# Large matmuls that read and write their 512 columns as two interleaved halves, with stationary arrays moved by 64 to 192 bytes

## The reference, cut to what matters

```
proj = rms_norm(x) @ gla_w_in       # 2048 -> 6160
x   += o @ gla_w_out                # 2048 -> 2048
x   += (silu(g) * u) @ ffn_w_out    # g, u = split(rms_norm(x) @ ffn_w_in): 2048 -> 2 * 5632, then 5632 -> 2048, twice
kv   = rms_norm(x) @ w_kv           # 2048 -> 4096
q    = rms_norm(x) @ diff_w_q       # 2048 -> 2048
x   += attention @ diff_w_out       # 2048 -> 2048
```

## Time and profile before

| what | value |
|---|---|
| median of the runs | 2196.01 us (2 runs, 2195.74 to 2196.29) |
| span of the profiled execution, first to last instruction | 2193.8 us |
| time of a run outside that span | 2.2 us (the median less the span) |
| TensorE busy | 2188.1 us, 9720 matmuls |
| weight loads busy | 1808.9 us |
| VectorE, ScalarE, GpSimd busy | 1242.7, 1058.2, 283.0 us |
| moved by DMA | 447.01 MB, mean 204 GB/s |

### The profile page before, as it was taken

The page is one execution under the profiler, slowest core; times in us unless marked ns, Lnnn a source line. Parts: engine busy times, 40 slices in busy tenths (PEclk is TensorE's granted clock), DMA queues, the critical chain, the costliest instruction groups (busy, mean ns, idle before and its releaser), DMA issues.

```text
span 2193.8 us, 27239 instructions
## 1 busy us (share of the span) xinstructions
PE 2188.1 (100%) x9720; PEld 1808.9 (82%) x9720; DVE 1242.7 (57%) x1460; ACT 1058.2 (48%) x1428; POOL 283.0 (13%) x563
## 2 busy tenths in 40 slices
PE   9999999999999999999999999999999999999999
PEld 7888788888888888888888888888888888888887
DVE  5665566655555555555566676665555555555443
ACT  6666455444444444444456665554444444444333
POOL 3210334100000000001125333341000000000000
PEclk9999999999999999999999999999999999999999
DMA  8765667666666666666667666676666666666664
GB/s 264 210 189 176 189 202 218 203 215 203 203 202 213 201 202 206 200 205 203 201 202 217 196 207 202 204 223 210 199 207 200 215 200 203 205 210 194 195 193 163
DMA packets 252675, 447.01 MB, mean 204 GB/s; under 512 B 27665, under 2 KB 41969, under 8 KB 252593
## 3 DMA queue, kind: packets, MB, share of 16 engines
q1 hardware_dynamic: 236176, 428.79, 62.2%
q0 software_dynamic: 16240, 17.07, 2.7%
q10 hardware_dynamic: 176, 0.07, 0.0%
HBM read 414.37 MB, written 2.10 MB: 190 GB/s over the span
## 4 chain that ended last, share of the span: by engine, by line
PE 100%; DVE 0%; ACT 0%; issue 0%; POOL 0%; DVEq 0%; ACTq 0%; POOLq 0%
PE acc L641 32%; PE acc L639 32%; PE acc L640 32%; PE acc L651 1%; PE acc L656 0%; PE side L884 0%; PE tps L678 0%; PE side L727 0%; PE side L703 0%; PE side L762 0%; PE side L882 0%; PE side L898 0%; PE side L899 0%; PE side L900 0%; PE side L782 0%; PE side L780 0%
## 5 line engine op out<-in xcount | busy, mean ns | idle before, releaser
L1311 DVE TENSOR_TENSOR w_lo<-raw,w_hi 128x1024 fp32r<-128x1024 f32 x784 | 954.8, 1222 | 835.6 <-ACT w_hi L945 831.3
L945 ACT ACTIVATE w_hi<-raw 128x1024 fp32r<-128x1024 f32 x784 | 827.8, 1059 | 1002.9 <-PE acc L641 994.0
L639 PE MATMUL acc<-w_hi,xT 128*128 128x512 f32 x2016 | 787.6, 391 | 0.0
L641 PE MATMUL acc<-w_hi,xT 128*128 128x512 f32 x2016 | 784.4, 389 | 0.0
L640 PE MATMUL acc<-w_lo,xT 128*128 128x512 f32 x2016 | 784.4, 389 | 0.0
L639 PEld LDWEIGHTS acc<-w_hi,xT 128*128 128x128 f32 x2016 | 378.4, 188 | 79.0 <-issue 0.7
L640 PEld LDWEIGHTS acc<-w_lo,xT 128*128 128x128 f32 x2016 | 378.4, 188 | 78.9 <-issue 0.7
L641 PEld LDWEIGHTS acc<-w_hi,xT 128*128 128x128 f32 x2016 | 378.4, 188 | 78.9
L639 PE MATMUL acc<-w_hi,hT 128*128 128x512 f32 x700 | 272.3, 389 | 0.0
L640 PE MATMUL acc<-w_lo,hT 128*128 128x512 f32 x700 | 272.3, 389 | 0.0
L641 PE MATMUL acc<-w_hi,hT 128*128 128x512 f32 x700 | 272.3, 389 | 0.0
(11 more groups left out here) (204 smaller groups left out, 1372.2 us busy)
## 6 DMA issues: line engine op xcount, KB each, us to landing
raw<-in_ffn_w_in SPq DMA_DIRECT2D x352, 512.0 KB, 3.8
raw<-in_ffn_w_out SPq DMA_DIRECT2D x176, 512.0 KB, 4.7
raw<-in_gla_w_in SPq DMA_DIRECT2D x96, 512.0 KB, 4.3
raw<-in_w_kv SPq DMA_DIRECT2D x64, 512.0 KB, 4.6
raw<-in_gla_w_out SPq DMA_DIRECT2D x32, 512.0 KB, 4.9
raw<-in_diff_w_q SPq DMA_DIRECT2D x32, 512.0 KB, 4.6
raw<-in_diff_w_out SPq DMA_DIRECT2D x32, 512.0 KB, 4.9
tok<-scratch SPq DMA_DIRECT2D x352, 32.0 KB, 2.9
```

What stands on the lines that cost most here:

```text
L639: nc.tensor.matmul(acc[p][tb][:, :], hi, w_hi[:, slot, j, :], start=(kt + j == 0), stop=False)
L641: last = nc.tensor.matmul(acc[p][tb][:, :], lo, w_hi[:, slot, j, :], start=False, stop=(kt + j == n_kt - 1))
L945: nc.scalar.activation(w_hi[:, slot, :, :], raw[:, slot, :, :], ACT.Copy).then_inc(hi_done, 1)
L1311: nc.vector.tensor_tensor(w_lo[:, slot, :, :], raw[:, slot, :, :], w_hi[:, slot, :, :].bitcast(F32), ALU.subtract).then_inc(lo_done, 1)
```

## The change

In `unit`, the moving operand (`w_hi`, `w_lo`) and the output bank are seen as two halves of 256 columns, which are walked in turn: c columns of the low half, c of the high half, the next c of the low half, and so on. Input and output are walked alike, so each product still lands in its own column. The number c depends on the phase: 4, 8, 16 or 32. `first_unit` and `last_unit` keep the straight walk. The number, order and operands of the matmuls and weight loads stay, as do all waits and DMAs. Beside that, the arrays `g_oT`, `hT`, `xT_q` and `d_oT` start at 64, 128, 128 and 192 bytes modulo 512, in place of 0; `xT` stays at 0. What lies behind them in SBUF (`x_turned`, `q_squares`, `p_squares`, `p_turned`) moves along.

```diff
-            place("gap_g", 0, s1)
+            place("gap_g", 64, s1)
             g_oT = sb("g_oT", [P, 2, KT, S], F32R, s1)
...
-            place("gap_h", 0, s1)
+            place("gap_h", 128, s1)
             hT = sb("hT", [P, 2, FKT, S], F32R, s1)
...
-            place("gap_d", 0, s1)
+            place("gap_q", 128, s1)
             with ExitStack() as s2:
                 xT_q = sb("xT_q", [P, 2, KT, S], F32R, s2)
+            place("gap_d", 192, s1)
             d_oT = sb("d_oT", [P, 2, KT, S], F32R, s1)
...
+            chunk = {'gla_in': 16, 'gla_out': 16, 'ffn_in0': 4, 'ffn_out0': 16, 'diff_in': 8, 'diff_q': 8, 'diff_out': 16, 'ffn_in1': 32, 'ffn_out1': 4}
+
+            def halves(row, c):
+
+                if c == CB:
+                    return row
+                return row.rearrange("q (h m c) -> q m h c", h=2, c=c)
+
-            def unit(src, kt, n_kt, p, slot, u):
+            def unit(src, kt, n_kt, p, slot, u, c=CB):
...
-                        nc.tensor.matmul(acc[p][tb][:, :], hi, w_hi[:, slot, j, :], start=(kt + j == 0), stop=False)
-                        nc.tensor.matmul(acc[p][tb][:, :], hi, w_lo[:, slot, j, :], start=False, stop=False)
-                        last = nc.tensor.matmul(acc[p][tb][:, :], lo, w_hi[:, slot, j, :], start=False,
-                                                stop=(kt + j == n_kt - 1))
+                        at, high, low = (halves(row, c) for row in (acc[p][tb][:, :], w_hi[:, slot, j, :], w_lo[:, slot, j, :]))
+                        nc.tensor.matmul(at, hi, high, start=(kt + j == 0), stop=False)
+                        nc.tensor.matmul(at, hi, low, start=False, stop=False)
+                        last = nc.tensor.matmul(at, lo, high, start=False, stop=(kt + j == n_kt - 1))
```

More of the change, by code:

```diff
@@ L819, in _ @@
                     u = UNIT0["gla_in"] + b * UB + k
-                    (first_unit if b == 0 else unit)(xT, 2 * k, KT, b % 2, u % SLOTS, u)
+                    if b == 0:
+                        first_unit(xT, 2 * k, KT, b % 2, u % SLOTS, u)
+                    else:
+                        unit(xT, 2 * k, KT, b % 2, u % SLOTS, u, chunk["gla_in"])
             def out_phase(phase, src, n_kt, units, before, src_job=None):
@@ L833, in out_phase @@
                     u = UNIT0[phase] + at
-                    (last_unit if u == UNITS - 1 else unit)(src, 2 * k, n_kt, b % 2, u % SLOTS, u)
+                    if u == UNITS - 1:
+                        last_unit(src, 2 * k, n_kt, b % 2, u % SLOTS, u)
+                    else:
+                        unit(src, 2 * k, n_kt, b % 2, u % SLOTS, u, chunk[phase])
             def turn_x(phase, b, x_name):
@@ L856, in ffn_pair @@
                         pe.wait_ge(evacuated[half], TB * (BLOCK0[phase] // 2) + TB * i)
-                    unit(xT, 2 * k, KT, half, at % SLOTS, UNIT0[phase] + 2 * UB * i + at)
+                    unit(xT, 2 * k, KT, half, at % SLOTS, UNIT0[phase] + 2 * UB * i + at, chunk[phase])
             def ffn(layer, x_name):
@@ L921, in _ @@
                     u = UNIT0["diff_in"] + b * UB + k
-                    unit(xT_q if 4 <= b < 8 else xT, 2 * k, KT, b % 2, u % SLOTS, u)
+                    if 4 <= b < 8:
+                        unit(xT_q, 2 * k, KT, b % 2, u % SLOTS, u, chunk["diff_q"])
+                    else:
+                        unit(xT, 2 * k, KT, b % 2, u % SLOTS, u, chunk["diff_in"])
             def diff_tail(at):
```

## The result

The changed kernel takes 2347.57 us (2 runs, 2347.55 to 2347.59) against 2196.01 before: a ratio of 1.069, with a 95% interval of 1.066 to 1.072. It is 152 us slower, where I forecast 70 us faster, and lies outside the range.

A forecast was written before the change was run, and what follows sets the result against it. TensorE's matmul pace was taken as the bound. From the 2193.8 us span, 70 us was taken off for the moving operand's walk, other parts adding nothing; with 2.2 us around it, 2126 us, range 2090 to 2215.

The forecast's parts named there:

- What bounds the kernel: Whole kernel: TensorE is busy for 2188.1 of 2193.8 us, so time is number of matmuls times distance between starts, 226.7 ns.
- What the 13.3 ns is made of: Each wide matmul's excess over 213.3 ns streaming: 2 ns fixed cost, 11.4 ns moving stream held up by the weight load.
- The walk of the moving operand: Reads of w_hi and w_lo in halves keep in step with the load: 7.5 ns gained on 9300 matmuls, 70 us.
- The walk of the output: PSUM bank written in pieces, smallest four float32: taken as costing nothing, though no row gave a price.
- my slow rival: The rival "Breaks cost", with 0.42 ns at each break of the output walk; chance 0.08.
- The new offsets: Stationary arrays moved to 64, 128 or 192 bytes: 3252 matmuls, plus or minus 4.4 ns, included in the 7.5 ns.
- No effect: Rival: the excess is what swapping 128 stationary columns takes; 2196 us. Chance 0.32, including gains or losses too small to matter.
- In step and always meeting: Rival: a bad offset makes each line meet; xT's 6048 matmuls at 236 ns cost 56 us, giving 2252 us; chance 0.06.
- Breaks cost: Rival: 604,000 breaks of the walk at 0.42 ns cost 252 us, giving 2448 us, or 2378 with the gain; chance 0.08.

## Why the prediction was wrong

- **What bounds the kernel** was right: TensorE throughout, time = count x pace. The 152 us are the pace of 9300 matmuls and nothing else: the sum over the phases closes. Issue, waits, DMA and the other engines stayed hidden, as costed.
- **What the 13.3 ns is made of** was half wrong. That the place of the stationary against the moving rows matters was read rightly from the earlier trace rows and is shown by the offset kernels. That the surplus is the load holding up the stream in proportion to what it reads was not: it doesn't fall with fewer loaded columns. The smaller excess of the 96-column group in the earlier trace rows was taken for an effect of fewer columns and of place; at 96 columns and 512 wide the pace is (68 + 0.39) / 297 = 230.3 ns, above the 226.7 of 128 columns. The 113.3 ns over four of that group came from a row rounded to 10 ns: by the recorded starts these four are 115.0 ns apart, single distances in the group are 112 to 121, and the bound of 4.4 ns drawn from it had little under it. That identical matmuls cost other amounts at another timing was read rightly; the two paces of one walk bear it out.
- **The walk of the moving operand** is the step that failed, in sign. I took 7.5 ns of gain for keeping the stream in step with the load. It cost 10.0 to 23.4 ns instead, all of it on the reading side: with the walk on the reading alone the kernel takes 2347.98 us, on the writing alone no more than the offsets do. It costs this whether 128 or 64 columns are loaded (c = 16) and wherever the stationary rows start. The row that could have given a price was missing: no matmul of that trace read in pieces, and I bounded the price only by rows of straight reads, 0.24 us at the worst, where 0.25 was measured at c = 4. Why broken reads cost what they do stays open.
- **The walk of the output** at nothing was right, to 0.1 ns, though my slow rival put its price there. By the Trainium skill (PSUM — Partial Sum Buffer, Specifications (TRN2)) a non-contiguous pattern slows matmuls significantly; the trace of the kernel that walks only the writing, in pieces of four float32, doesn't agree, at 226.6 ns.
- **The new offsets** were given plus or minus 4.4 ns. They cost 5.7 to 6.7 ns with the straight walk (19 us) and nothing with the walk. The list of their units names the 88 of a feed-forward output once; both have to be counted, 88 + 88 + 32 + 32 + 32 less one, and the 3252 does count them.
- **The rivals.** "No effect" was out by 152 us, and what speaks against it is that moving the stationary rows alone takes the straight walk from 226.7 to 233.3 ns. The Trainium skill (TensorE: Matmul & The Clock Gate, Part 2, step 1) has independent read ports for the two operands, so that a weight load takes no read bandwidth from the running matmul; that leaves no room for this effect of place, and the measurement decides. "In step and always meeting" would have spared `hT`; it didn't. "Breaks cost" named the sign that came, ffn_in0 far slower than ffn_in1 (250.1 against 236.6), and its price of 0.42 ns per break gave 252 us where 152 came. The price per break isn't constant, the reading side pays it, and eight breaks are free. I had let the reading side off because four float32 make two hits and more per line. That rule of the Trainium skill (SBUF — State Buffer, Door 1) asks for two hits per 16-byte line; the runs don't agree, for pieces of four float32, a whole line, cost 23.4 ns, and pieces of two, still two hits if each float32 is one, cost 113.
- **What stays open.** Which addresses collide with which: a table of piece and jump was measured, and neither a price per break nor a return to the same place modulo 256 bytes explains all of it. Also open is what makes one walk run at two paces. The runs show that it isn't the walk, the array or its place, and once a stop of 0.42 us changed it in mid-phase. Whether the timing against the weight loads counts or that against the other engines, no run tells apart.

## What to carry to other kernels

Where TensorE's own pace is the bound, read it as count per window and compare it with the streaming time, but don't book the surplus as gain on a mechanism that no row isolates: measure pieces, offsets and loaded columns in a kernel that gives each phase a setting of its own. For float32r matmuls like these, leave the moving operand in straight stretches of 64 float32 or more, and keep stationary and moving rows 0 or 256 bytes apart modulo 512. Distrust a mechanism that rests on differences of a few nanoseconds in rows rounded to ten. Before a reordered access is taken, split it into its reading and its writing half; here one was free and the other cost 152 us.

## What the runs showed of the hardware

- A float32r matmul of 512 columns ran at 226.7 ns with straight reads and stationary rows at 0 or 256 bytes from the moving rows modulo 512, and at 228.9 to 233.3 ns at the other eight distances tried (32, 64, 128, 192, 224, 384, 448, 480).
- Writes to PSUM in pieces of four float32 were free; reads from SBUF in two halves cost 10.0, 13.3, 16.7, 23.4 and 113 ns per matmul for pieces of 32, 16, 8, 4 and 2 columns, and nothing from 64 columns up. At four columns the cost also depends on how far apart the parts lie: 267.8 and 276.1 ns for 512 and 256 bytes, against 250.0 for 1024.
- Some walks ran faster than the straight one (220.0 ns over 65 us, 223.3 over 468 us) and have several stable paces: 220.0 and 230.7 ns for one, 223.3 and 226.7 for another. A stop of 0.42 us took the second from 223.3 to 226.7 ns.
- By the recorded starts many steady paces (220.0, 223.3, 226.7, 230.0, 233.3, 236.7, 240.0, 243.3, 250.0, 340.0, 443.3 ns) lie whole steps of 3.33 ns apart, about the time in which eight columns stream (213.3 / 64; an estimate). Others, such as 228.9, 232.4 and 276.1, don't, and no run says why.
- The kernels with such walks scatter from run to run, 2186.8 to 2199.3 us for one and 2184.9 to 2191.6 for the other, where the kernel before stays within 2 us.
